# RWKV-7 mix, first stage: the four projections as three f32r products each

## The reference, cut to what matters

```python
def rwkv7_time_mix(h, ...):                    # h: 1024 tokens x 1024
    xx = token_shift(h) - h
    lerp = lambda j: h + xx * mu[j]
    xr, xw, xk, xv, xa, xg = (lerp(j) for j in range(N_LERP))
    r, k, v, g = xr @ w_in[0], xk @ w_in[1], xv @ w_in[2], xg @ w_in[3]   # each 1024 x 2048
    w_log = -jax.nn.softplus(-(w0 + jnp.tanh(xw @ w1) @ w2)) - 0.5
    decay = jnp.exp(-jnp.exp(w_log))
    a = jax.nn.sigmoid(a0 + (xa @ a1) @ a2)
    ...
    y = wkv7_scan(...)        # per head of 64: S = S diag(w) - (S kk)(a kk)^T + v k^T;  y = S r
    y = (head_group_norm(y) + bonus) * jax.nn.silu(g)
    return y @ w_out
```

## Time and profile before

| | |
|---|---|
| three timed runs | 4592.5, 4591.0, 4587.2 us; median 4591.0 |
| the profiled execution's own time | 4586.5 us |
| its span | 4584.8 us |
| TensorE busy (products) | 4219.0 us, 92% |
| TensorE weight loads | 3217.2 us, 70% |
| VectorE | 2370.4 us, 52% |
| ScalarE | 1315.9 us, 29% |
| GpSimd | 274.1 us, 6% |
| first stage in the span | about 0 to 2163 us |
| weight transfers `a_wt` | 256 of 512 KB, 4.2 us from issue to landing |

### The profile page before, as it was taken

How to read it: one execution, slowest core, us unless ns; L and a number is a source line. 1 busy time by engine, 2 the same in 40 slices (tenths; PEclk the granted TensorE clock), 3 DMA queues, 4 the chain that set the end, 5 groups by cost and what they waited for, 6 DMA issues and landing times. The chain is left out here.

```text
span 4584.8 us, 131580 instructions
## 1 busy us (share of the span) xinstructions
PE 4219.0 (92%) x58346; PEld 3217.2 (70%) x58346; DVE 2370.4 (52%) x5302; ACT 1315.9 (29%) x3044; POOL 274.1 (6%) x308
## 2 busy tenths in 40 slices
PE   7999999999999999998988999999969977877579
PEld 5888888888888888886777887888746643444344
DVE  4556555565555655554215543444255533688842
ACT  2233323332323223222213332232113312433221
POOL 1000000000000000000000000000000000111100
PEclk9999999999999999998999999999989988566789
DMA  2322222222222222221413333333211110000010
GB/s 74 92 68 79 63 88 68 83 64 78 77 79 68 79 68 77 70 79 50 127 37 110 96 96 83 101 96 96 55 42 28 23 37 9 1 1 0 0 46 37
DMA packets 520412, 289.54 MB, mean 63 GB/s; under 512 B 30256, under 2 KB 509728, under 8 KB 519904
## 3 DMA queue, kind: packets, MB, share of 16 engines
q1 hardware_dynamic: 519904, 281.88, 21.3%
HBM read 267.55 MB, written 12.58 MB: 61 GB/s over the span
## 5 line engine op out<-in xcount | busy, mean ns | idle before, releaser
L344 PE MATMUL a_bank<-a_lerps,a_wt 128*128 128x256 f32 x4096 | 1036.9, 393 | 2.4 <-DVE a_lerps L815 2.4
L344 PEld LDWEIGHTS a_bank<-a_lerps,a_wt 128*128 128x128 f32 x4096 | 731.0, 189 | 126.9 <-issue 21.2
L1208 PE MATMUL b_bank<-b_hR,b_wR 128*128 128x512 f32 x1024 | 399.8, 390 | 15.5 <-DVE b_wL L1213 15.5
L1208 PE MATMUL b_bank<-b_hL,b_wR 128*128 128x512 f32 x1024 | 399.7, 390 | 0.0
L1208 PE MATMUL b_bank<-b_hR,b_wL 128*128 128x512 f32 x1024 | 399.5, 390 | 0.0
L931 DVE TENSOR_TENSOR a_iv_X<-a_bank,a_iv_X 128x256 f32<-128x256 f32 x256 | 108.7, 425 | 413.3 <-PE a_bank L448 413.3
L1213 DVE TENSOR_TENSOR b_wL<-b_w,b_wR 128x1024 fp32r<-128x1024 f32 (+1 forms) x144 | 192.4, 1340 | 116.8 <-ACT b_wR L1296 104.0
L692 ACT ACTIVATE a_iv<-a_bank 128x512 f32<-128x512 f32 x192 | 114.7, 597 | 419.1 <-PE a_bank L454 266.2
L1208 PEld LDWEIGHTS b_bank<-b_hR,b_wR 128*128 128x128 f32 x1024 | 193.0, 188 | 56.0 <-issue 16.1
L1208 PEld LDWEIGHTS b_bank<-b_hL,b_wR 128*128 128x128 f32 x1024 | 192.9, 188 | 40.4
L1208 PEld LDWEIGHTS b_bank<-b_hR,b_wL 128*128 128x128 f32 x1024 | 193.0, 189 | 40.2
(11 more groups left out here) (441 smaller groups left out, 8156.7 us busy)
## 6 DMA issues: line engine op xcount, KB each, us to landing
a_wt<-in_a_w_in SPq DMA_DIRECT2D x256, 512.0 KB, 4.2
b_w<-in_b_w_in SPq DMA_DIRECT2D x128, 512.0 KB, 4.0
b_w<-in_b_w_out SPq DMA_DIRECT2D x16, 1024.0 KB, 5.6
rwkv_out<-a_ybuf SPq DMA_DIRECT2D x64, 128.0 KB, 5.7
m_w<-in_a_w_out SPq DMA_DIRECT2D x16, 512.0 KB, 4.0
s_wp<-in_w_in SPq DMA_DIRECT2D x12, 512.0 KB, 3.8
a_xtok<-in_x SPq DMA_DIRECT2D x4, 1024.0 KB, 7.1
m_two<-rwkv_out SPq DMA_DIRECT2D x16, 256.0 KB, 3.0
```

What stands on the lines that cost most here:

```text
L344: r = mm(o, wt[:, j, c, :], src[:, c, :], start=(c == 0), stop=(c == ND - 1))
L1208: m = nc.tensor.matmul(o, a, b, start=(first and i == 0), stop=(last and i == 2))
```

## The change

Each of the four projections is made of three f32r products a chunk: `wR` with `lerpR`, `wR` with `lerpL`, `wL` with `lerpR`, into the same bank as before, in the same nine runs a step. For each group ScalarE rounds the four weight tiles (128x1024) to `wR` and VectorE subtracts to get `wL`. For each pass, the lerps are made in 16 units of two chunks: VectorE writes a unit (128x512) to one of three buffers `tmp`, ScalarE rounds it to `lerpR`, GpSimd subtracts to get `lerpL`. There is one set of lerps instead of two, so a unit is written only when the last use of the old one is done; for that, the lerps move from steps 10 to 13 to steps 14 and 15 (and run on into the use of them in step 15, which already projects the first group of the next pass). The shifted differences take the space of `xtok` and are all made in step 13. SP's waits and order change, the state's store moves to the start of the next step.

Changed parts, cut to the core ("..." marks what is left out):

```diff
 # SP
                 for m in range(STEPS):
-                    sp.wait_ge(s["prk"], m + 1)
-                    ...
+                    for i, name in enumerate(LERPS):          # LERPS = "krgv"
+                        if m:
+                            sp.wait_ge(s["wL"], (m - 1) * len(LERPS) + i + 1)
+                        sp.dma_start(wt[name][:, :, :], w_in[W_IN[name]][:, :, cols]).then_inc(s["w" + name], 16)
+                        if i == 0:
+                            if m:
+                                sp.wait_ge(s["pwa"], m)
+                            sp.dma_start(lwa2[w_rows, :], ...).then_inc(s["low"], 16)
+                            sp.dma_start(lwa2[a_rows, :], ...).then_inc(s["low"], 16)
+                    if m >= 4:
+                        store(m - 4)
 # TensorE
+                def project(o, m, name, lo, hi):
+                    if lo == 0:
+                        pe.wait_ge(s["wL"], m * len(LERPS) + LERPS.index(name) + 1)
+                    if m % NF == 0:
+                        pe.wait_ge(s["lo"], unit(m // NF, name, (hi + 1) // 2 - 1) + 1)
                     for c in range(lo, hi):
-                        r = mm(o, wt[:, j, c, :], src[:, c, :], start=(c == 0), stop=(c == ND - 1))
+                        mm(o, wR[name][:, c, :], lerpR[name][:, c, :], start=(c == 0), stop=False)
+                        mm(o, wR[name][:, c, :], lerpL[name][:, c, :], start=False, stop=False)
+                        r = mm(o, wL[name][:, c, :], lerpR[name][:, c, :], start=False, stop=(c == ND - 1))
 # ScalarE
+                def round_weights(m, names=LERPS):
+                    for name in names:
+                        act.wait_ge(s["w" + name], 16 * (m + 1))
+                        sem, count = free(name, 0)
+                        act.wait_ge(s[sem], count + m)
+                        a(wR[name][:, :, :], wt[name][:, :, :], ACT.Copy).then_inc(s["wR"], 1)
+                def round_lerp(ps, name, i):
+                    n = unit(ps, name, i)
+                    act.wait_ge(s["tmp"], n + 1)
+                    sem, count = free(name, ps)
+                    act.wait_ge(s[sem], count)
+                    a(lerpR[name][:, 2 * i:2 * i + 2, :], tmp[n % 3][:, :, :], ACT.Copy).then_inc(s["hi"], 1)
 ...  step:
                         rates(m, e)
+                    lerps(15, ("r", 2), ("r", 3), ("g", 0))
                     ...                                        # copies S2E2, S4E4
                         decays(m, e)
+                    lerps(15, ("g", 1), ("g", 2), ("g", 3))
                     ...                                        # copy E8
                         keys(m, e)
+                            round_weights(m + 1, "k")
                     ...                                        # copies ZY, trVK, Z, Y, W0
                         bonus(m, e)
+                            round_weights(m + 1, "r")
                         gate(m, e)
+                    lerps(14, ("k", 0), ("k", 1), ("k", 2))
+                    lerps(15, ("v", 0), ("v", 1), ("v", 2), ("v", 3))
                     act.wait_ge(s["pP12"], ready)
                     copy_two(pr12, 4, "P12", scale=-1.0)
+                    lerps(14, ("k", 3), ("r", 0), ("r", 1))
                     ...
+                            round_weights(m + 1, "g")
                         vals(m, e)
+                            round_weights(m + 1, "v")
 # GpSimd
+                def low_lerp(ps, name, i):
+                    n = unit(ps, name, i)
+                    pool.wait_ge(s["hi"], n + 1)
+                    low(lerpL[name][:, pair_of, :], tmp[n % 3][:, :, :], lerpR[name][:, pair_of, :]).then_inc(s["lo"], 1)
 ...  step: step 14 has k0 to k3, r0, r1; step 15 has r2, r3, g0 to g3, v0 to v3; both after root(n - 1), before bonus(m)
 ...        step 13 has the eight shift(prep, c) after bonus(m)
 # VectorE
+                def lerped(ps, *units):
+                    for name, i in units:
+                        n = unit(ps, name, i)
+                        v.wait_ge(s["xx"], ps * ND + 2 * i + 2)
+                        if n >= 3:
+                            v.wait_ge(s["lo"], n - 2)
+                        for c in (2 * i, 2 * i + 1):
+                            o = stt(tmp[n % 3][:, c % 2, :], xx[:, c, :], mu, hT[:, c, 1:PASS + 1], ALU.mult, ALU.add)
+                        o.then_inc(s["tmp"], 1)
+                def low_weights(m, names):
+                    for name in names:
+                        v.wait_ge(s["wR"], m * len(LERPS) + LERPS.index(name) + 1)
+                        tt(wL[name][:, :, :], wt[name][:, :, :], wR[name][:, :, :].bitcast(F32), ALU.subtract).then_inc(s["wL"], 1)
 ...  step:
                         columns(m, e2, m % NF)
+                        low_weights(m, "gv")
+                    if prep and at == 15:
+                        lerped(prep, ("g", 1), ("g", 2), ("g", 3))
                     add_to_x("X2", "pX2", "X1")
                     ...
                         bonus_keys(m, e2)
+                    if prep and at == 14:
+                        lerped(prep, ("k", 0), ("k", 1), ("k", 2))
+                    if prep and at == 15:
+                        lerped(prep, ("v", 0), ("v", 1), ("v", 2))
                     ...
                         gate(m, e2)
+                            low_weights(m + 1, "kr")
+                    if prep and at == 14:
+                        lerped(prep, ("k", 3), ("r", 0), ("r", 1))
+                    if prep and at == 15:
+                        lerped(prep, ("v", 3))
                     ...                                        # G, H, R, four state updates
+                    if prep and at == 14:
+                        lerped(prep, ("r", 2), ("r", 3), ("g", 0))
```

More of the change, by code:

```diff
@@ L139, in rwkv_block @@
         hT = sb("hT", [P, ND, PASS + 1])
-        lerps = sb("lerps", [P, 2, 4, ND, PASS])
-        lerp = [{n: lerps[:, b, i, :, :] for i, n in enumerate("rkvg")} for b in range(2)]
-        wt = sb("wt", [P, 4, ND, P])
+        lerpR, lerpL = ({n: sb(f"lerp{x}_{n}", [P, ND, PASS], F32R) for n in "krgv"} for x in "RL")
+        wR, wL = ({n: sb(f"w{x}_{n}", [P, ND, P], F32R) for n in "krgv"} for x in "RL")
+        tmp = [sb(f"tmp{i}", [P, 2, PASS]) for i in range(3)]
+        wt = {n: sb(f"wt_{n}", [P, ND, P]) for n in "krgv"}
         lwa2 = sb("lwa2", [2 * LORA, P])
@@ L261, in steps, with unit, free @@
                 step(n, n % 2, n % NF, n + 1 if n + 1 < STEPS else None, n - 1 if n else None)
+        LERPS = "krgv"
+        MU = {"r": 0, "k": 2, "v": 3, "g": 5}
+        W_IN = {"r": 0, "k": 1, "v": 2, "g": 3}
+        UNITS = len(LERPS) * ND // 2
+        def unit(ps, name, i):
+            return ps * UNITS + LERPS.index(name) * (ND // 2) + i
+        def free(name, ps):
+            return {"k": ("pk", ps * NF), "r": ("prk", ps * NF + 1), "g": ("pg", ps * NF + 1), "v": ("pv", ps * NF + 1)}[name]
         def prepared(n):
@@ L332, in low_rank @@
                 def low_rank(m):
-                    pe.wait_ge(s["wk"], (m + 1) * 48)
+                    pe.wait_ge(s["low"], (m + 1) * 32)
                     pe.wait_ge(s["bdR"], m + 1)
@@ L413, in first @@
                         turn_x(0, i, 2 + i)
-                    pe.wait_ge(s["wk"], 48)
                     low_in(0, 0, ND, 6)
-                    for c in range(ND):
-                        keys(m, c, c + 1)
+                    for c in range(0, ND, 2):
+                        keys(m, c, c + 2)
                     low_rank(m)
-                    pe.wait_ge(s["lerps"], ND)
-                    gate(m, 0, ND)
-                    receptance(m, 0, ND)
-                    vals(m, 0, ND)
+                    for c in range(0, ND, 2):
+                        receptance(m, c, c + 2)
+                    for c in range(0, ND, 2):
+                        gate(m, c, c + 2)
+                    for c in range(0, ND, 2):
+                        vals(m, c, c + 2)
                     key_norm(m)
@@ L673, in first @@
                         turned_x(0, i, 2 + i)
-                    low_out(0, 6)
-                    rates(m, e)
-                    decays(m, e)
+                    for name in LERPS:
+                        for i in range(ND // 2):
+                            if i == 0:
+                                round_weights(m, name)
+                            round_lerp(0, name, i)
+                        if name == "k":
+                            low_out(0, 6)
+                            rates(m, e)
+                            decays(m, e)
                     keys(m, e)
@@ L692, in copy_two, with lerps @@
                         return a(tiles[:, :, :, :].rearrange("p w a b -> p (w a b)"), bank[bk][:, :], ACT.Copy, scale=scale).then_inc(s[done], 1)
+                    def lerps(at_step, *units):
+                        if prep and at == at_step:
+                            for name, i in units:
```

(17 more changed lines are left out.)

84 lines of the change are left out of this document (38 added, 46 removed).

## The result

The changed kernel is slower. Its median is 4629.4 us over four runs, against 4589.1 us for the kernel before in the same session: ratio 1.0086, interval 1.0069 to 1.0104. The forecast was 4477 us, faster; the time lies outside the range and on the other side of no change. None of the four rivals in it had the mechanism that decided.

What follows compares the result with a forecast made beforehand. TensorE was taken to bound the first stage, busy 2087 of 2098 us. Products -165, passes +45 and start +6 gave -114 us, from 4591.0 to 4477 us, range 4425 to 4560.

Steps and rivals of the forecast that it cites:

- The products: Projection runs: 96 f32r products at 0.118 us replace 32 chunks of 0.436; 2.62 us a step, -165 us in all.
- Rivals 3 and 4: Projection runs: 3, f32r no cheaper at 256 columns, 4590, chance 0.04; 4, load and stream in series, 5094, chance 0.07.
- rival 2: Every step: the value copy or -P1/-P2 comes late behind a rounding, +63 us, 4540; chance 0.06.
- Transfers, "Cost 0": SP's queue: same 2 MB a step, each load released by its buffer's low part, landing in about 4 us; cost 0.
- Rounding and low weights, cost 0: Each step: four ScalarE roundings (4.2 us) and four VectorE subtractions (4.9 us) fit into idle time; cost 0.
- The passes: Steps 14 and 15: lerps, roundings and GpSimd subtractions cost 15 us a pass, three passes, +45 us.
- S2/E2: Step 15: this ScalarE copy stands behind three roundings and ends at 9.3 us, TensorE wants it at 5.8: +3.5 us.
- E8: Step 15: this ScalarE copy for TensorE waits behind three further roundings: +1.2 us.
- -P1/-P2: Step 15: this ScalarE copy stands behind four value roundings, the fourth waiting for VectorE: +4 us.
- 5 of 15: End of each pass: 5 of the 15 us were for GpSimd and VectorE getting in each other's way.
- The start: Ahead of the loop: rounding and subtracting for all four projections come in series with their products, +6 us (2 to 14).
- rival 1: Passes and start: each GpSimd subtraction stops VectorE for its whole 1.30 us, 31 us a pass, 4533; chance 0.18.

Runs made afterwards that it cites:

- e1_spread: The changed kernel with its weight transfers set apart: r ahead of the low-rank loads, g after the receptance, v after the gate projection; 4528.6 us, ratio 0.9873.
- e3_old_burst: The kernel before the change, plus three unread 512 KB loads a step, one behind the other after the low-rank product; 4686.9 us, ratio 1.0205.
- e5_edge: e1_spread with ScalarE's S2/E2, E8 and -P1/-P2 copies in step 15 moved ahead of roundings; 4532.4 us, ratio 0.9878.
- e9_short_low: e7_edge_v with the low parts at the end of each pass computed for only 16 of 256 columns; 4487.6 us in one run.
- e7_edge_v: e5_edge plus the start of e4_first_order, with v0, v1 and v2 rounded earlier by ScalarE in step 15; 4511.2 us, ratio 0.983.
- e4_first_order: The changed kernel reordered ahead of the loop only: lerps' low parts on VectorE instead of GpSimd, low weights earlier, keys' work before values; 4616.1 us, ratio 1.0057.

## Why the prediction was wrong

- **The products: right.** Records 0.12 us apart, shortest steps 29.9 us against 29.8 forecast. Rivals 3 and 4 are out; rival 2, a late tile in every step, is too. The Trainium skill, TensorE: Matmul & The Clock Gate, Part 3, has weight loads overlap products in flight only in another row group; f32r products on the same rows, each with its own load, follow each other at 0.12 us, and the trace goes against that rule again.
- **Transfers, "Cost 0": this step failed.** The prediction checked when each load is needed and when it lands; none is late. It did not ask what else goes over the DMA engines while three loads and a store are under way together, nor compare the spacing of the requests with the old one. TensorE's own instructions go there, 256 to a packet, and came late. "r at some 3 us of the step, g and v at some 6" stood in it, and nothing was drawn from that. Measured: about 2.3 us a common step, 130 us in all; e1_spread, which only spaces the same requests, gives 101 of them back, and e3_old_burst makes 98 in the old kernel with a burst alone. Of the 2.3 us, 1.4 are stops (82 over 57) and some 0.5 the granted clock (28 over 57), which is 0.62 behind the stop at 1270 us; e1_spread loses under 1 us by the clock in all its common steps.
- **Rounding and low weights, cost 0: right in common steps.** TensorE waits for no wL there and for no P12 (two short waits for P12, 0.8 us, stand in steps 15), and e1_spread comes to 30.45 us a step with all of them in.
- **The passes: +45 forecast, 53 measured** with the stops that fall into them, 48 in e1_spread. The size is near, but by luck: the terms differ. The forecast waits are there (S2/E2, E8), and -P1/-P2 hardly; instead TensorE waits for GpSimd's value low parts, 4.7 us in step 15. All its waits in that step are 10.2 us of the 15.5 over the expected length; the other 5 go with the granted clock (0.11 of 45.2 us, an estimate), 0.89 over the step where the kernel before has 1.00, and no term of the forecast had that. e5_edge removed most of ScalarE's waits and gained nothing, since VectorE was as late. e9_short_low shows that in e7_edge_v GpSimd carries over half of what is left, where I had put its share at 5 of 15.
- **The start: +6 forecast, +24 measured.** The size was off. I had 21 us of GpSimd subtractions, but not that VectorE's lerps beside them take 0.92 us instead of 0.44, and put too little on the products waiting for the low weights (10.1, 4.3 and 4.0 us for r, k and g ahead of the loop). e4_first_order gets 14 of the 24 back.
- **GpSimd and VectorE.** The case I gave 0.18 (rival 1) was nearer than mine where lerps stand beside subtractions: 0.92 - 0.44 is 0.48 us for each lerp, about 1 us for each subtraction of 1.3. I had judged by the start of the kernel before, where subtractions were short and few. The Trainium skill, SBUF — State Buffer, Who interferes with whom, says that a VectorE operation with two SBUF inputs and a GpSimd one that reads SBUF exclude each other; these rows agree, and also the low weights, which take 2.12 and 2.28 us beside GpSimd in step 15 and 1.22 elsewhere.

The change loses 40 us, and the spacing of four DMA requests costs it 101. With that mended it wins 60 us over the kernel before (e1_spread, against 4589 in its session), with the start and step 15 reordered 78 (e7_edge_v, 1.7%). Of the 165 us of the products, the rest stays in the passes, the start and small stops.

## What to carry to other kernels

When an edit moves the points at which buffers come free, write down when each transfer will be asked for, before and after, and not only whether it lands in time. Several transfers of half a megabyte asked for together can stop an engine that needs none of them, where it runs through many short instructions; put them apart, or where its instructions are long. A wait after "issue" in the middle of a group of identical instructions is the sign; hold its end against the q8 packets. And when one late engine's order is mended, read the next trace for who is late in its place before counting the gain.

## What the runs showed of the hardware

- Instruction packets share the DMA engines with data. In the loop 16 to 21 packets of 16 KB come in 100 us, one for every 256 records of TensorE. With the data queues at a share of 1.1 to 1.2 and 330 to 350 GB/s, TensorE stopped within a group of identical products, for 1.9 us at 1205.9 and 2.5 us at 239.8. All 69 such waits of the changed kernel and all 47 of e3_old_burst end 1.2 to 1.6 us after a packet has ended. The Trainium skill, SBUF — State Buffer, Who interferes with whom, says that DMA never contends with a compute engine. For the ports that may be so, no run here shows otherwise; for the time of the engine it misleads, as +98 us from loads that nobody reads show.
- A share of about 0.9 for 6 us did no harm where the trace has 41 to 55 records of TensorE in 2 us; a share over 1.1 went with a stop where it has 105. At the same density, 256 records in 3.4 us, the packet began 1.1 us after their first with hardly any traffic and 2.5 us with the burst.
- A stop of 2.5 us is followed by a granted clock of 0.63 and 0.52 in the next stretches of 2 us, a stop of 1.6 us by 0.62 for 3 us, and the one of 1.9 us at 1205.9 by none (1.00). Of the 32 stops of over 1 us in the loop of the changed kernel 16 were followed by the lower level, and 11 of these were longer than 2 us.
- A GpSimd subtraction of 128x512 takes 1.3 us, on VectorE 0.68. Moving it there pays ahead of the loop (-13 us) and loses in step 15 (+20 us): what counts is whose list stands on the way back to TensorE.
